# First expert table split by columns: 896 columns multiplied densely, 1152 gathered

## The chip, the core and the metric

One core of a Trainium2 chip runs the whole kernel in one launch. The metric is device time in microseconds (us), lower is better. All arithmetic is float32 (or fp32r, a float32 that PE reads in one pass).

## What is computed

A first block (retention, latent attention) and the attention of a second block come first; the change doesn't touch them. Behind them stands a mixture of 16384 experts, of which each of 256 tokens takes 8 heads x 16 picks = 128:

```python
q = (xt @ w_query).reshape(T, 8, 2, 128)
scores = jnp.einsum('thpc,hpnc->thpn', q, sub_keys)
vals, idx = lax.top_k(scores, 16)                      # per half: 16 of 128 keys
cand = (vals[..., 0, :, None] + vals[..., 1, None, :]).reshape(T, 8, 256)
top_vals, top_c = lax.top_k(cand, 16)
experts = i1 * 128 + i2                                # i1, i2: keys of the two halves
gates = softmax(top_vals)
# xc: tokens after rms_norm and gain
u = jnp.take(expert_down, experts, axis=0)             # rows of 2048
hdn = gelu(einsum('ted,td->te', u, xc))
vsel = jnp.take(expert_up, experts, axis=0)            # rows of 2048
y = einsum('te,ted->td', gates * hdn, vsel)
out = rms_norm(h + y)
```

## The kernel before

Tokens lie as two tiles t of 128 on the partitions. SP streams all weight matrices through eight 4 KB slots in the order of a list (`plan`); PE multiplies them as three fp32r products of high and low parts; ACT makes the high part, DVE the low one. Each engine's program is written out in order, with semaphores named for what was made (`x.at(key)` is waited for, `x.to(key)` is signalled). `take(b)` on PE waits until PSUM bank b is free.

The expert part, engine by engine:

**Selection.** PE multiplies queries with keys (`sel_scores`, L2200). ACT copies the scores to `SC`; the copy for tile 1 waits until tile 0 is ranked there. DVE ranks them (`top16`, `select`, L1584 to L1658) as a list of small steps, 147 and 150 counting the gates: 73 run before the first row, then two before each row. `chosen` releases the row numbers `EI` of 64 picks, L1649 ends a tile's selection.

**First table.** POOL gathers one pick of 128 tokens per instruction (L640): 128 rows of 2048 columns into one of NG = 8 buffers, for 256 picks. DVE multiplies each with `HN` (the normed tokens with gain) and sums it into a column of `HD[t]` (L1686). At the end of a tile ACT takes the gelu (L1024), DVE multiplies by the gates (L1691): `coef_made`.

**Second table, 896 columns (`DCOL`) by a dense product.** The coefficients of a tile are spread over all 16384 experts: PE turns `HD` (L2248), and for each group q of four tokens two one-hots of 128 are made, the first weighted by the coefficients, and multiplied with each other (`built`, L2258); ACT stores the result to `CO` (`store`, L1016). In tile 0 PE compares the picks' keys with 0..127 (two fp32r matmuls L2229 of 512 columns and two of one row, L2231) and ACT makes both one-hots (L1043 to L1053), beside the rows of tile 1. In tile 1 PE compares only the first key (L2229, L2231), DVE makes the first one-hot (L1707) after every second row of the second table, ACT the second (L1037, L1048). SP streams 128 blocks of 448 KB through NS = 4 slots, and PE multiplies each with both tiles' `CO` in four matmuls of 448 columns (L2275), once both tiles are stored.

**Second table, the other 1152 columns.** POOL gathers them (L651) into NU = 5 buffers; DVE adds coefficient times row to `X` (L1699), 256 rows one after another.

**End.** DVE adds the dense result (L1715), ACT squares, DVE scales, SP writes out.

Of the kernel before, what the change touches and what calls it, by code (L numbers as in the profile page):

```python
# [15 lines left out]
NG = 8  # L16
DCOL = 896
HCOL = DCOL // 2
NU = 5
# [15 lines left out]
K_ALL = 2066  # L35


def tables():
# [37 lines left out]
    t[:, K_STEP:K_ALL] = np.arange(128)  # L76
# [41 lines left out]
def build(nc, A, out):  # L118
    ctx = ExitStack()
    with ctx:  # L120
# [112 lines left out]
        HN = XN  # L233
        QT = at(YG + 4096, 16, 256)
        KT = at(W, 16, 128)
        SC = at(W + 2048, D)

        def column(o):
            cell = [o]

            def take_(*shape):
                a = at(cell[0], *shape)
                cell[0] += int(np.prod(shape))
                return a, cell[0]
            return take_

        scratch, kept = column(W + 4096), column(192 * KB + K_DM)
# [3 lines left out]
        WK, scratch_end = scratch(256)  # L251
        assert scratch_end <= 192 * KB, scratch_end
        II = [GBA[:, 128 * i:128 + 128 * i] for i in range(2)]
        IF = [GBA[:, 256 + 128 * i:384 + 128 * i] for i in range(2)]
        EI, GT, HD, CFT = ([kept(*n)[0] for _ in range(2)] for n in ((128,), (8, 16), (128,), (128,)))
        GS = kept(8)[0]
        G16, kept_end = kept(128)
        EF = [GBA[:, 512 + 256 * t:768 + 256 * t].rearrange("p (i j) -> p i j", i=2) for t in range(2)]
        EFR = [at(kept_end + 256 * t, 2 - t, 128, of=arena_r) for t in range(2)]
        SECOND = at(kept_end + 384, 128)  # L260
        STEP, LESS, IDR, ONER = (at(kept_end + 512 + 128 * i, 128, of=arena_r if i else arena) for i in range(4))
        assert kept_end + 1024 <= LBO + 4 * 384, kept_end
        gbuf = [at(RAWS + i * 2048, D) for i in range(NG)]

        ubuf = [at(W + 4096 + (D - DCOL) * i, D - DCOL) for i in range(2)] + [at(YG + (D - DCOL) * i, D - DCOL) for i in range(3)]
        sbuf = [at(144 * KB + DCOL * i, DCOL) for i in range(2)] + [at(W + 8192 - DCOL * i, DCOL) for i in (2, 1)]
        OH1 = [at(152 * KB + 512 * i, 4, 128) for i in range(2)]
        OH2 = [at(152 * KB + 1024 + 512 * i, 4, 128) for i in range(2)]

        CO = [[(0, 64, at(16 * KB, 64, 128)), (64, 32, at(YG + 4096, 32, 128)), (96, 32, at(W, 32, 128))],  # L270
              [(0, 64, at(RAWS, 64, 128)), (64, 64, at(HLS, 64, 128))]]

        def coef_of(t, i2):
            return next(ap[:, i2 - a, :] for a, n, ap in CO[t] if a <= i2 < a + n)

# [149 lines left out]
        d_g = [dma_sig(f"d_g{i}", range(32)) for i in range(NG)]  # L425
        d_u = [dma_sig(f"d_u{i}", range(52)) for i in range(NU)]
        d_s = [dma_sig(f"d_s{i}", range(43)) for i in range(NS)]
# [82 lines left out]
        sel_ranked = sig("sel_ranked", [(t, f) for t in range(2) for f in range(2)])  # L510
        chosen = sig("chosen", [(t, f) for t in range(2) for f in range(2)])
        gate_in, gate_exp, gate_made = sig("gate_in", range(2)), sig("gate_exp", range(2)), sig("gate_made", range(2))
        rows_used = sig("rows_used", range(512))
        gelud, coef_made = sig("gelud", range(2)), sig("coef_made", range(2))
        rounded, picks_rounded = sig("rounded", [0]), sig("picks_rounded", range(2))
        coef_turned, coef_copied = sig("coef_turned", range(2)), sig("coef_copied", range(2))
        fours = [(t, q) for t in range(2) for q in range(32)]
        first_hot_a, first_hot_v = sig("first_hot_a", fours[0:32]), sig("first_hot_v", fours[32:])
        compared, less_read, second_hot = sig("compared", fours), sig("less_read", fours), sig("second_hot", fours)
        second_turned, second_copied = sig("second_turned", [0]), sig("second_copied", [0])  # L520
        built, stored = sig("built", fours), sig("stored", fours)
        block_used = sig("block_used", range(127))
# [33 lines left out]
        down, up_rows, up_blocks = A["peer_down_2"][0], A["up_rows"], A["up_blocks"]  # L556


        def sync(sp):
# [22 lines left out]
            sp.wait_ge(*gate_made.at(1))  # L582
            sp.wait_ge(*picks_rounded.at(1))
            sp.wait_ge(*second_copied.at(0))
# [10 lines left out]
        def gpsimd(g):  # L595
# [33 lines left out]
            g.dma_start(GBB, A["ffn_norm_gain_2"][0].partition_broadcast(128)).then_inc(*d_ff.to("all"))  # L629
            g.dma_start(STEP, A["table"][:, K_STEP:K_ALL]).then_inc(*d_step.to("all"))  # L630
            g.dma_start(G16[0:16, :], A["final_norm_gain_2"].rearrange("(n p) -> n p", p=128)).then_inc(*d_f2.to("all"))

            g.wait_ge(*query_copied.at((3, 1)))
            for n in range(256):
                i, t, j = n % NG, n // 128, n % 128
                if j % 64 == 0:
                    g.wait_ge(*chosen.at((t, j // 64)))
                if n >= NG:
                    g.wait_ge(*rows_used.at(n - NG))
                g.indirect_dma_start(  # L640
                    out=gbuf[i], out_offset=None, in_=down,
                    in_offset=bass.IndirectOffsetOnAxis(ap=EI[t][:, j:j + 1].bitcast(U32), axis=0)
                ).then_inc(*d_g[i].to(n // NG))
            g.wait_ge(*gate_made.at(1))
            for n in range(256):
                i, t, j = n % NU, n // 128, n % 128
                if n == 2:
                    g.wait_ge(*rows_used.at(255))
# [8 lines left out]
        def scalar(s):  # L657
# [361 lines left out]
            for t in range(2):  # L1019
# [9 lines left out]
                for q in range(33):  # L1029
# [25 lines left out]
                    if q:  # L1055
                        store(t, q - 1)
# [1258 lines left out]
```

## Time and profile before

| | us |
|---|---|
| median of three runs | 3309.46 (3308.81 to 3310.41) |
| profiled execution, its own time | 3310.61 |
| its span | 3308.8 |
| PE busy | 2507.0 (76%) |
| DVE busy | 2292.5 (69%) |
| ACT busy | 1032.7 (31%) |
| POOL busy | 871.4 (26%) |

The core moved 866.75 MB, mean 262 GB/s. Times in the rows are us from the start of the span unless marked ns. PE is TensorE's matmuls, PEld its weight loads, DVE VectorE, ACT ScalarE, POOL GpSimd, SP the queue of SyncE. "Clock" is the share of 2.4 GHz that TensorE was granted. A float32 matmul leaves two records, an fp32r one leaves one. Durations of PE records include the way through the array; how often they come is read from their number in a stretch. A gather's duration on POOL is its issue alone.

### The profile page before, as it was taken

How to read it: one execution, taken by the hardware profiler on the slowest of the kernel's cores; microseconds unless marked ns; L12 is line 12 of the kernel's file. 1: busy time of each engine (PE TensorE's matmuls, PEld its weight loads, DVE VectorE, ACT ScalarE, POOL GpSimd, SP SyncE). 2: the span in 40 equal slices, each digit the busy share in tenths (PEclk: the TensorE clock that was granted, in tenths of full speed). 3: DMA queues.
4: the chain of work that ended last, by engine and by line, in shares of the span. 5: the costliest groups of instructions: out<-in, count | busy, mean ns of one | idle time of the engine just before them, and what ended most of it. 6: DMA issues, size and time to landing. Idle time of an engine off the chain costs nothing.

```text
span 3308.8 us, 34747 instructions
## 1 busy us (share of the span) xinstructions
PE 2507.0 (76%) x13253; PEld 2029.7 (61%) x13253; DVE 2292.5 (69%) x3034; ACT 1032.7 (31%) x1748; POOL 871.4 (26%) x581
## 2 busy tenths in 40 slices
PE   3689999998989998799999986000069106899995
PEld 3689999996879986698888786000036004655552
DVE  6877777776765455533435557999999898866666
ACT  2234343434344444443335442000058105400000
POOL 5510000000000000000000002833388786744444
PEclk9789999998989999799989988555555555599997
DMA  8767787775856534355333543999999998999998
GB/s 291 254 232 244 262 272 261 257 258 198 294 177 172 152 115 134 110 165 164 103 90 109 165 151 148 382 367 347 338 407 422 420 422 318 323 407 409 410 409 318
DMA packets 340694, 866.75 MB, mean 262 GB/s; under 512 B 38072, under 2 KB 97728, under 8 KB 306864
## 3 DMA queue, kind: packets, MB, share of 16 engines
q1 hardware_dynamic: 265872, 439.15, 40.1%
q0 software_dynamic: 74656, 425.38, 33.0%
q8 instruction: 105, 1.72, 0.2%
q14 instruction: 61, 0.50, 0.0%
HBM read 862.34 MB, written 2.10 MB: 261 GB/s over the span
## 4 chain that ended last, share of the span: by engine, by line
PE 35%; DVE 14%; DMA 12%; POOL 11%; issue 4%; ACT 1%; DVEq 0%; ACTq 0%; POOLq 0%
DMA s<-in_up_rows,s 10%; PE ps L1741 10%; PE ps L1742 10%; PE ps L1743 10%; POOL s L640 8%; DVE s L1686 7%; POOL s L651 3%; DVE s L1699 2%; DMA s<-in_peer_down,s 1%; PE ps L2119 1%; PE ps L2002 1%; PE ps L2121 1%; DVE s L1596 0%; DVE s L1587 0%; DVE s L1590 0%
## 5 line engine op out<-in xcount | busy, mean ns | idle before, releaser
L1741 PE MATMUL ps<-r,r 128*128 128x256 f32 (+2 forms) x3248 | 1063.9, 328 | 74.7 <-DVE r L1089 43.5
L1742 PE MATMUL ps<-r,r 128*128 128x256 f32 (+2 forms) x3248 | 1044.5, 322 | 0.0
L1089 DVE TENSOR_TENSOR r<-s,r 128x1024 fp32r<-128x1024 f32 (+1 forms) x532 | 647.3, 1223 | 572.9 <-ACT r L666 572.5
L1743 PE MATMUL ps<-r,r 128*128 128x256 f32 (+2 forms) x3248 | 1043.3, 321 | 0.0
L666 ACT CAST r<-s 128x1024 fp32r<-128x1024 f32 (+1 forms) x532 | 550.3, 1039 | 897.7 <-PE ps L1743 849.9
L1741 PEld LDWEIGHTS ps<-r,r 128*128 128x128 f32 x3248 | 639.9, 197 | 132.7 <-DVE r L1089 41.2
L1742 PEld LDWEIGHTS ps<-r,r 128*128 128x128 f32 x3248 | 640.4, 197 | 43.0 <-issue 4.6
L1743 PEld LDWEIGHTS ps<-r,r 128*128 128x128 f32 x3248 | 639.2, 197 | 41.0
L1686 DVE CUSTOM_DVE_ANT_0 s<-s,s 128x2048 f32<-128x2048 f32 x256 | 582.8, 2285 | 33.2 <-DMA s<-in_peer_down,s 33.0
L640 POOL DMA_INDIRECT s<-in_peer_down,s x256 | 464.8, 1816 | 409.6 <-DVE s L1644 189.3
L1699 DVE SCALAR_TENSOR_TENSOR s<-s,s,s 128x1152 f32<-128x1152 f32 x256 | 363.0, 1418 | 167.0 <-DMA s<-in_up_rows,s 162.9
L651 POOL DMA_INDIRECT s<-in_up_rows,s x256 | 305.0, 1191 | 253.4 <-DVE s L1699 205.7
L2275 PE MATMUL ps<-s,s 128*128 128x448 f32 x960 | 366.0, 542 | 0.0
L2229 PE MATMUL ps<-r 128*128 128x512 f32 x96 | 75.0, 781 | 353.8 <-ACT r L1010 353.8
L2275 PEld LDWEIGHTS ps<-s,s 128*128 128x128 f32 x960 | 183.3, 191 | 179.6 <-issue 179.6
L625 POOL DMA_DIRECT2D s<-in_final_norm_g x1 | 0.6, 625 | 1093.0 <-DVE s L1435 1093.0
L2229 PEld LDWEIGHTS ps<-r 128*128 128x128 f32 x96 | 30.5, 318 | 368.0 <-ACT r L1007 354.0
L1107 DVE SCALAR_TENSOR_TENSOR s<-s,s,s 128x512 f32<-128x512 f32 x304 | 226.8, 783 | 2.5 <-DMA s<-in_ada_w 1.1
L2248 PE MATMUL ps<-s 128*128 128x128 f32 x2 | 0.9, 448 | 202.5 <-DVE s L1691 202.5
L2258 PE MATMUL ps<-s 128*128 128x128 f32 x512 | 131.9, 439 | 27.9 <-issue 17.1
L2258 PEld LDWEIGHTS ps<-s 128*128 128x128 f32 x512 | 114.0, 328 | 56.9 <-ACT s L1016 29.3
L1060 ACT ACTIVATE s<-s 128x1152 f32<-128x1152 f32 x2 | 2.3, 1162 | 419.1 <-DVE s L1699 419.1
(266 smaller groups left out, 2033.7 us busy)
## 6 DMA issues: line engine op xcount, KB each, us to landing
s<-in_ada_w SPq DMA_DIRECT2D x192, 512.0 KB, 5.3
s<-in_ret_w_in SPq DMA_DIRECT2D x128, 512.0 KB, 5.2
s<-in_up_blocks SPq DMA_DIRECT2D x128, 448.0 KB, 6.8
s<-in_w_in SPq DMA_DIRECT2D x96, 512.0 KB, 3.7
s<-in_ret_w_in SPq DMA_DIRECT2D x128, 256.0 KB, 3.8
s<-in_ret_w_out SPq DMA_DIRECT2D x64, 512.0 KB, 5.0
s<-in_mla_w_in SPq DMA_DIRECT2D x48, 512.0 KB, 3.7
s<-in_mla_w_out SPq DMA_DIRECT2D x32, 512.0 KB, 3.6
```

The costliest lines, as they stand in the source:

```text
L640: g.indirect_dma_start(out=gbuf[i], out_offset=None, in_=down, in_offset=bass.IndirectOffsetOnAxis(ap=EI[t][:, j:j + 1].bitcast(U32), axis ...
L651: g.indirect_dma_start(out=ubuf[i], out_offset=None, in_=up_rows, in_offset=bass.IndirectOffsetOnAxis(ap=EI[t][:, j:j + 1].bitcast(U32), a ...
L666: s.copy(hi_of(w), raw_of(w)).then_inc(*hi_made.to(w))
L1089: v.tensor_tensor(lo_of(w), raw_of(w), hi_of(w).bitcast(F), ALU.subtract).then_inc(*lo_made.to(w))
L1107: r = v.scalar_tensor_tensor(out=acc[h], in0=w, scalar=cact[:, k:k + 1], in1=acc[h], op0=ALU.mult, op1=ALU.add)
L1686: v.tensor_tensor_reduce(gbuf[n % NG], gbuf[n % NG], HN[:, t, :], 1.0, 0.0, ALU.mult, ALU.add, HD[t][:, j:j + 1]).then_inc(*rows_used.to(n))
L1699: v.scalar_tensor_tensor(out=X[:, t, DCOL:], in0=ubuf[n % NU], scalar=HD[t][:, j:j + 1], in1=X[:, t, DCOL:], op0=ALU.mult, op1=ALU.add).th ...
L1741: pe.matmul(o, lh, rh, start=start, stop=False, skip_group_check=True)
L1742: pe.matmul(o, lh, rl, start=False, stop=False, skip_group_check=True)
L1743: return pe.matmul(o, ll, rh, start=False, stop=stop, skip_group_check=True)
L2258: r = pe.matmul(bank[b][:, k * 128:(k + 1) * 128], OH1[q % 2][:, k, :], OH2[q % 2][:, k, :], start=True, stop=True)
L2275: r = pe.matmul(bank[2 * t + b][:, 0:HCOL], coef_of(t, i2), sbuf[i2 % NS][:, b * HCOL:(b + 1) * HCOL], start=i2 == 0, stop=i2 == 127)
```

## The change

The first table is split like the second. `down_rows` holds columns 896 to 2047, `down_blocks` the other 896, as 128 blocks, one for each first key i1, laid out as [128 columns of a part, 7 parts, 128 second keys i2].

- **Dense product.** SP streams the 128 blocks through the four slots that later hold the second table's (now 256 blocks in a row; the first two wait for `hn_made`, the next two for the last scores). After the scores PE multiplies each with the normed tokens `XNT` (transposed, kept from the turning of "E"), 7 matmuls of 256 columns a block, two blocks a bank. ACT copies the result to `DH[i2, i1 group, token, i1]`, 64 copies.
- **Picks.** After the last copy, for each group q of four tokens of a tile: PE spreads the tokens' second keys over the partitions (`spread_`, four matmuls of 128 columns, one bank), ACT turns them into a one-hot (`pick_hot_`: Abs, Relu), PE multiplies it with the four tokens' slices of `DH` (`pick_rows`, four matmuls of 512 columns in all), so that each pick has its 128 values over i1, and DVE takes the one at its first key (`pick`, four operations on PSUM with a sum) into `SL`. PE turns `SL`, DVE adds it to `HD` (`hidden`), then gelu and gates as before.
- **Order.** DVE calls `pick` for tile 0 after rows 116 to 147, one a row, for tile 1 after rows 150, 153, ..., 243. PE runs tile 0's 32 groups after the dense product; in tile 1's loop it also builds tile 0's coefficients, three groups behind, with a single pair of one-hot buffers. ACT likewise.
- **Rows.** Gathers of both tables have 1152 columns. The first 56 use a ring of NA = 7 buffers, all later ones a ring of NB = 4. Row 56 waits for the end of selection. The second table's rows follow in the same ring.
- **Selection.** Five steps before each row; `SC` has a buffer for each tile; the gates are made after rows 64 and 100. `HNG`, the tokens times gain, has 1152 columns.

```diff
-NG = 8
-NU = 5
+GCOL = D - DCOL
+NA, EARLY, NB = 7, 56, 4
...
+        def before_row(n):
+            return n - NA if n < EARLY + NB else n - NB
+        PICK_AT = [116 + q for q in range(32)] + [150 + 3 * q for q in range(32)]
...
-            for b in range(128):
+            for b in range(256):
+                if b == 0:
+                    sp.wait_ge(*hn_made.at(1))
+                if b == 2:
+                    sp.wait_ge(*sel_scored.at((1, 3)))
                 if b >= NS:
                     sp.wait_ge(*block_used.at(b - NS))
-                sp.dma_start(sbuf[b % NS], up_blocks[b]).then_inc(*d_s[b % NS].to(b // NS))
+                sp.dma_start(sbuf[b % NS], down_blocks[I1_ORDER[b]] if b < 128 else up_blocks[b - 128]).then_inc(
+                    *d_block[b % NS].to(b // NS))
...
+            for q in pairs64:
+                if q in (20, 40):
+                    picks(q // 20 - 1)
+                s.wait_ge(*block_used.at(2 * q + 1))
+                if q == 32:
+                    s.wait_ge(*gate_in.at(1))
+                if q == 48:
+                    s.wait_ge(*rows_used.at(EARLY - 1))
+                i1 = I1_ORDER[2 * q]
+                s.copy(DH[:, i1 // 32, :, i1 % 32:i1 % 32 + 2], bank[4 + q % 4].rearrange("p (i t) -> p t i", i=2)).then_inc(
+                    *hid_stored.to(q))
+
+            def pick_hot_(t, q):
+                o = flat(PH[q % 2])
+                s.wait_ge(*spread.at((t, q)))
+                if fours.index((t, q)) >= 2:
+                    s.wait_ge(*rows_picked.at(fours[32 * t + q - 2]))
+                s.activation(o, bank[2], ACT.Abs, bias=NEG).then_inc(*spread_read.to((t, q)))
+                s.wait_ge(*spread_read.at((t, q)))
+                s.activation(o, o, ACT.Relu, scale=-1.0, bias=1.0).then_inc(*pick_hot.to((t, q)))
...
+            def pick(t, q):
+                if q == 0:
+                    v.wait_ge(*turned_read.at(t))
+                v.wait_ge(*rows_picked.at((t, q)))
+                for k in range(4):
+                    o, c = bank[3 + q % 2][:, k * 128:(k + 1) * 128], 4 * q + k
+                    r = v.scalar_tensor_tensor(out=o, in0=STEP, scalar=FIRST[t][:, c:c + 1], in1=o, op0=ALU.is_equal,
+                                               op1=ALU.mult, accum_out=SL[t][:, c:c + 1])
+                r.then_inc(*picked.to((t, q)))
...
             for n in range(256):
                 t, j = n // 128, n % 128
                 if n:
-                    next(choice, None)
-                    next(choice, None)
-                v.wait_ge(*d_g[n % NG].at(n // NG))
-                v.tensor_tensor_reduce(gbuf[n % NG], gbuf[n % NG], HN[:, t, :], 1.0, 0.0, ALU.mult, ALU.add,
+                    for _ in range(5):
+                        next(choice, None)
+                v.wait_ge(*d_row[row_slot(n)[1]].at(n))
+                v.tensor_tensor_reduce(row_buf(n), row_buf(n), HNG[:, t, :], 1.0, 0.0, ALU.mult, ALU.add,
                                        HD[t][:, j:j + 1]).then_inc(*rows_used.to(n))
+                if n in (64, 100):
+                    gates((64, 100).index(n))
+                if n == 148:
+                    hidden(0)
+                if n == 150:
+                    coefficients(0)
+                if n in PICK_AT:
+                    pick(*fours[PICK_AT.index(n)])
+            hidden(1)
+            coefficients(1)
...
+            for q in pairs64:
+                if q in (20, 40):
+                    turn_picks(q // 20 - 1)
+                take(4 + q % 4)
+                for j in range(2):
+                    b = 2 * q + j
+                    pe.wait_ge(*d_block[b % NS].at(b // NS))
+                    w = sbuf[b % NS].rearrange("p (k i) -> p k i", i=128)
+                    for k in range(DCOL // 128):
+                        r = pe.matmul(bank[4 + q % 4][:, j * 256:(j + 1) * 256], w[:, k, :], XNT[:, k, :],
+                                      start=k == 0, stop=k == DCOL // 128 - 1)
+                    r.then_inc(*block_used.to(b))
+                free[4 + q % 4] = hid_stored.at(q)
+
+            def spread_(t, q):
+                if q == 0:
+                    pe.wait_ge(*picks_rounded.at(t))
+                take(2)
+                for k in range(4):
+                    r = pe.matmul(bank[2][:, k * 128:(k + 1) * 128], IDR[:, 4 * q + k:4 * q + k + 1].broadcast_to([128, 128]),
+                                  EFR[t][:, 1, :], start=True, stop=True)
+                r.then_inc(*spread.to((t, q)))
+                free[2] = spread_read.at((t, q))
+
+            def pick_rows(t, q):
+                b = 3 + q % 2
+                take(b)
+                pe.wait_ge(*pick_hot.at((t, q)))
+                for k in range(4):
+                    c = 128 * t + 4 * q + k
+                    r = pe.matmul(bank[b][:, k * 128:(k + 1) * 128].rearrange("p (c i) -> p c i", c=4), PH[q % 2][:, k, :], DH[:, :, c, :], start=True, stop=True)
+                r.then_inc(*rows_picked.to((t, q)))
+                free[b] = picked.at((t, q))
...
             pe.wait_ge(*rounded.at(0))
...
+            pe.wait_ge(*hid_stored.at(63))
+            spread_(0, 0)
+            for q in range(32):
+                if q < 31:
+                    spread_(0, q + 1)
+                pick_rows(0, q)
+            spread_(1, 0)
+            for q in range(32):
+                if q < 31:
+                    spread_(1, q + 1)
+                pick_rows(1, q)
+                if q == 0:
+                    turn_picked(0)
+                if q == 2:
+                    turn_coef(0)
+                    compare(0, 0)
+                if q >= 3:
+                    build_(0, q - 3)
+                    compare(0, q - 2)
...
```

## Rows read from the trace of the kernel before

**Rows 1.** Busy time by stretch; busy us and (count) of each engine, clock, DMA.

```profile
core 0: us, PE busy (x) PEld busy (x) DVE busy (x) ACT busy (x) POOL busy (x), PEclk, DMA share, GB/s
1950.00:2000.00 50.00, 50.00 (x420) 50.00 (x420) 24.08 (x34) 20.07 (x24) 0.00 (x0) 1.00 0.57 179
2042.00:2745.00 703.00, 149.43 (x388) 92.15 (x388) 665.48 (x850) 136.85 (x368) 469.17 (x258) 0.50 0.98 386
2049.00:2389.00 340.00, 0.00 (x0) 0.00 (x0) 335.58 (x556) 2.25 (x5) 176.98 (x116) 0.50 0.96 362
2430.00:2590.00 160.00, 143.45 (x379) 89.76 (x379) 146.66 (x131) 128.31 (x347) 136.10 (x66) 0.50 1.01 421
2745.70:2880.10 134.40, 108.67 (x352) 79.53 (x352) 119.25 (x104) 78.47 (x225) 105.34 (x74) 0.50 0.91 314
2880.10:3267.50 387.40, 387.40 (x1025) 195.42 (x1024) 240.54 (x171) 1.25 (x2) 180.16 (x169) 0.99 1.02 406
2900.00:2950.00 50.00, 50.00 (x134) 25.27 (x133) 29.79 (x21) 0.00 (x0) 19.24 (x22) 1.00 1.02 408
```

**Rows 2.** Groups by line from 2000 us to the end.

```profile
L1686 DVE DVE_READ_ACCUMULATOR2_ANT s<- 128x1 f32 x256 | 21.1, 82 | 0.0
L1707 DVE SCALAR_TENSOR_TENSOR s<-ps,s 128x512 f32<-128x512 f32 x32 | 21.9, 684 | 0.0
L1691 DVE TENSOR_TENSOR s<-s 128x128 f32<-128x128 f32 x2 | 0.6, 294 | 0.8 <-ACT s L1024 0.8
```

**Rows 3.** Single lines: count, shortest/median/longest ns, first and last start.

```profile
L2200 PE MATMUL ps<-s,s x64: 272/275/341, 1989.2 to 2036.6; 128*128 128x128 f32 x64
L640 POOL DMA_INDIRECT s<-in_peer_down,s x256: 935/2170/3010, 2043.2 to 2726.2; - x128
L1649 DVE TENSOR_TENSOR s<-s x2: 293/294/294, 2161.7 to 2388.9; 128x128 f32<-128x128 f32 x2
L1686 DVE CUSTOM_DVE_ANT_0 s<-s,s x256: 2239/2289/2353, 2049.2 to 2742.6; 128x2048 f32<-128x2048 f32 x128
L1699 DVE SCALAR_TENSOR_TENSOR s<-s,s,s x256: 1407/1419/1454, 2745.8 to 3291.5; 128x1152 f32<-128x1152 f32 x128
L2275 PE MATMUL ps<-s,s x960: 539/539/1115, 2880.1 to 3267.0; 128*128 128x448 f32 x192
```

**Rows 4.** Issue to landing (last, us): 2760 to 2875, then 2900 to 3200.

```profile
s<-in_up_rows,s POOLq DMA_INDIRECT x63, 6.6
...
s<-in_up_blocks SPq DMA_DIRECT2D x100, 448.0 KB, 6.8
s<-in_up_rows,s POOLq DMA_INDIRECT x131, 9.7
```

**Rows 5.** PE alone, two pauses: busy us (records), clock, DMA share, GB/s.

```profile
1252.00:1254.00 2.00, 0.07 (x1) 1.00 0.65 218
...
1274.00:1276.00 2.00, 0.00 (x0) 0.50 0.57 225
```

**Rows 6.** Timeline of one group of four in the first tile: PE, then ACT.

```profile
2432.32 0.77 PE L2229 MATMUL ps<-r 128*128 128x512 f32 x1
...
2435.19 2.08 PE L2258 MATMUL ps<-s 128*128 128x128 f32 x8
2436.92 0.77 PE L2229 MATMUL ps<-r 128*128 128x512 f32 x1
...
2435.30 0.60 ACT L1043 ACTIVATE s<-ps 128x512 f32<-128x512 f32 x1 [0.73 <-PE ps L2231]
...
2436.42 0.63 ACT L1047 ACTIVATE s<-s 128x512 f32<-128x512 f32 x1
...
2437.60 1.28 ACT L1053 ACTIVATE s<-s,s 128x128 f32<-128x128 f32 x4
2438.78 0.68 ACT L1016 COPY s<-ps 128x256 f32<-128x256 f32 x3
```

**Rows 7.** Timeline: first one-hot of the second tile.

```profile
2754.23 0.68 DVE L1707 SCALAR_TENSOR_TENSOR s<-ps,s 128x512 f32<-128x512 f32 x1
```

More of the change, by code:

```diff
@@ L267, in build @@
[L267 to L274, printed above, removed]
+        WK = scratch(256)[0]
+        II = [scratch(128)[0] for _ in range(2)]
@@ L1595, in top16 @@
                 v.wait_ge(*steps.at())
[L1596 removed]
+                v.max_index(idx[:, 8:16], val[:, 8:16], wk).then_inc(*steps.to())
                 yield
@@ L2219, in tensor, with turn_picks @@
                         sel_scores(t, g)
-            def compare(t, q):
+            def turn_picks(t):
+                pe.wait_ge(*chosen.at((t, 1)))
+                take(t)
+                for p in range(2):
+                    r = pe.transpose(bank[t][:, p * 128:(p + 1) * 128], EF[t][:, p, :], IDN)
+                r.then_inc(*picks_turned.to(t))
+                free[t] = turned_read.at(t)
+            for q in pairs64:
[11 more added lines that the diff above has]
+                free[4 + q % 4] = hid_stored.at(q)
@@ new lines, in turn_coef, with compare @@
+            def turn_coef(t):
+                take(5)
+                pe.wait_ge(*coef_made.at(t))
+                pe.transpose(bank[5][:, 0:128], HD[t], IDN).then_inc(*coef_turned.to(t))
+                free[5] = coef_copied.at(t)
+            def compare(t, q):
+                if t:
+                    b = q % 2
+                    if q == 0:
+                        take(0)
+                        take(1)
+                    take(b)
+                    hs = [(b, 0)]
+                else:
+                    hs = [(0, 0), (1, 1)]
+                    take(0)
+                    take(1)
+                for b, p in hs:
@@ new lines, in compare, with build_ @@
+                for b, p in hs:
+                    free[b] = first_hot_v.at((1, q)) if t else less_read.at((0, q))
+            def build_(t, q):
+                b = 6 + q % 2
+                take(b)
+                pe.wait_ge(*(first_hot_v if t else first_hot_a).at((t, q)))
+                pe.wait_ge(*second_hot.at((t, q)))
+                o1, o2 = (OH1[q % 2], OH2[q % 2]) if t else (OH1[0], OH2[0])
+                for k in range(4):
+                    r = pe.matmul(bank[b][:, k * 128:(k + 1) * 128], o1[:, k, :], o2[:, k, :], start=True, stop=True)
+                r.then_inc(*built.to((t, q)))
+                free[b] = stored.at((t, q))
@@ L2262, in tensor @@
+            for q in (29, 30, 31):
+                build_(0, q)
+                if q < 31:
+                    compare(0, q + 1)
+            turn_picked(1)
+            turn_coef(1)
+            compare(1, 0)
+            for q in range(32):
+                if q < 31:
+                    compare(1, q + 1)
+                build_(1, q)
             for b in range(4, 8):
```

308 lines of the change are left out of this document (153 added, 155 removed).

## The prediction

> **What bounds the kernel now.** I read the busy table by stretches first [rows 1]. Until 2037 us of the span it is projections and attention, which the change leaves alone. Then PE stops and the expert part begins: from 2042 to 2745 the core gathers whole 8 KB rows of the first expert table, DMA busy 0.98 at 386 GB/s, PE idle or at half clock. From 2745.7 to 2880 the first 1152-column rows of the second table are added while PE builds the second token tile's coefficients at clock 0.50. From 2880 to 3267 PE multiplies the 896-column blocks and is busy in every microsecond, with the DMA share at 1.02 and 406 GB/s: there both are full. The groups by line [rows 2] give prices, the sources' first and last starts [rows 3] the marks: gather issue begins at 2043.2, the second tile's selection ends at 2388.9 (L1649), the last first-table row starts on DVE at 2742.6, the first second-table row at 2745.75 (L1699), dense product 2880.1 to 3267, last row 3291.5. So the first-table stretch is limited by DMA (2.49 us a row late in it, by DVE steps before) and everything behind it hangs on one mark: **the moment T at which the coefficients of both tiles exist, now 2745.7.** From T to the end of the span it is 3308.8 - 2745.7 = 563.1 us. The change rewrites what comes before T and little behind it, so I compute the new T.
>
> **Bytes.** Removed: 256 gathers x 128 rows x 896 columns x 4 B = 117 MB. Added: 128 blocks of 448 KB = 59 MB. Net 58.7 MB less; at 386 GB/s that is 152 us, the most this can give if DMA stayed the bound. It does not: the rest of the sum is PE's.
>
> **Dense first product.** 128 blocks x 7 float32 matmuls with 256 moving columns. In the dense stage now, 134 records of 448 columns stand in 50 us [rows 1], 373 ns a record, two records a matmul: 0.833 ns per column and record. So 256 columns cost 427 ns, 896 matmuls 382 us, 2.99 us a block. What could hide or stall it: the scores end on PE at 2036.9 [rows 3], blocks 0 and 1 are loaded before, 2 and 3 land some 5 us later, in time. A slot comes round after three blocks, 9 us, against 6.8 us to landing [rows 4] beside saturated queues. The copies (64 of 512 columns, 0.68 us as three pieces in L1016's row [rows 6]) fit beside. Its 153 GB/s leaves the rows some 250 GB/s. PE comes from full clock (2.4 GHz), and the clock stays at 1.00 over a short gap: in [rows 5] PE worked 0.07 us of the two from 1252 on, and kept it; in a longer pause it had lost it by 1274. Weight loads lie beside the stream in [rows 1], 25 of 50 us. Dense ends at 2037 + 382 = 2419. In the Trainium skill, "TensorE: Matmul & The Clock Gate", section "What overlaps and what doesn't", a weight load overlaps running matmuls only where the row group differs; our loads take all rows, so by it this stage would be longer. The trace disagrees for this kind of matmul: 373 ns is two times 448 columns at 2.4 GHz with nothing between.
>
> **DVE and rows meanwhile.** 5 selection steps go before each row instead of 2; 221 steps remain. Now they and 110 rows take 2049 to 2389: 340 - 110 x (2.29 + 0.08) = 79 us for the steps; a little DMA wait is hidden in there, and as the steps' cost alone stands in no one row I take 92 between that and a third more, 105. With 45 rows of 1152 columns at 1.44 us (bounds: 2.29 x 1152/2048 = 1.29 and the 1.42 of L1699, plus 0.08 for reading the sum out) the selection is done near 2049 + 65 + 92 = 2206, before the copy that waits for it (pair 32, 2233). Rows then go at 2.3 us beside the stream; row 116, where DVE meets the first pick, comes near 2370. There it waits for PE until 2423: row gathers stop with it, and this is where the saved bytes go unused.
>
> **Picks of the first tile.** All on PE after the dense product. From its end to the first pick product: last copy 0.6, spread 0.5, Abs 0.6 and Relu 0.63 on ACT [rows 6] and hops, 3.5 us: 2423. Each group of four is 4 float32 matmuls of 512 columns: 4 x 853 = 3.41 us. The spread (4 matmuls fp32r of 128 columns) is not in the trace: below, 4 x 0.12 (the 256-column fp32r record, 420 in 50 us [rows 1]) = 0.5; above, 4 x 0.72 (the compare's cadence at half clock [rows 6]) = 2.9. I take 0.5, since it is the same array form as the former, without the one-row matmul between. So 3.9 us a group. ACT (1.2) and DVE (one row 1.44 + four picks) lie beside it; a pick is a 128-column operation on PSUM: below 4 x 0.29 (L1691, [rows 2]) = 1.2, above 4 x (0.68 + 0.08) = 3.1 from L1707 [rows 2]; I take 1.5. 32 x 3.9 = 125: 2548. Rows move one per group, 151 GB/s of the 406 possible.
>
> **Picks of the second tile, with the first tile's coefficients.** Three groups pass before the one-hots join (12 us) plus 4 us for transpose, gelu and coefficient copy one after another: 2564. Then per group PE does pick 3.41, spread 0.5, build 0.85 (8 records of 128 columns; 1.71 us at half clock [rows 6]), compare. The compare costs 2.87 us at half clock [rows 6], 0.72 a matmul, of which 0.43 is columns and 0.29 exposed load; at full clock 0.21 + 0.19, so 1.6. A hop to ACT's last one-hot copy adds 0.25: **6.6 us**. ACT needs 3.6 (from the first Abs at 2435.30 to the last copy's end at 2438.88 [rows 6]) + 0.6 + 1.2 = 5.4, DVE 3 x 1.44 + 1.5 = 5.8, both inside. 29 x 6.6 = 191: 2755. Twelve rows remain, four of them ready: 12 x 1.6 = 19; last pick, transpose, gelu and product 3 to 5. **T = 2779**, 33 us later than now. PE alone (382 + 125 + 191) already fills that stretch.
>
> **Behind T.** The same loops. Ring of 4 buffers for 5: in the one-hot stretch rows land 6.6 us after issue (median [rows 4]), so (6.6 + 1.42 + 0.1)/4 = 2.03 us a row against the present 1.87 (134.4 us for 72): at most 12 us; less if the queue in front is shorter. Against it, four rows lie ready at T, where now the first one-hot waits for late rows until 8.5 us after T [rows 7]. I put both together at nothing. In the dense stretch DMA is full whatever the ring. The store has one copy for two: nothing. Dropped norm columns, table loads: under 2 us, nothing.
>
> **Sum.** Span 3308.8 + 33 = 3342, and the profiled execution took 3310.6 for its 3308.8: 3344. It stood 1.2 us over the median of three, 3309.5, inside their spread, so I do not correct.
>
> **Rivals.**
> *Not slower: the loads hide at full clock (0.25).* If the compare costs its columns alone (0.85), a group takes 3.41 + 0.5 + 0.85 + 0.85 + 0.25 = 5.9, T is 2564 + 171 + 24 = 2759, and PE, still at full clock, leaves the later one-hot stretch to DVE (2 x 1.42 + 0.68, so 3.5 instead of 3.73 us a group, -7) with rows ready (-6): 3311; with a group of 3.6 in the first tile (-10) and the last rows at 1.44 (-2), 3299. It decides from T under 2751. For it: loads hide in the fp32r stream. Against: they did not in the compare, busy without a gap [rows 6]. Faster 0.15, same 0.10.
> *The ring of four limits the rows (0.12).* Now 9.7 us to landing + 1.42 + 0.3 make 11.4 for five, 2.28 a row. If landing stays 9.7, four give 2.85; 171 rows x 0.57 = 97 more: 3441. Against: the DMA share of 1.02 says that time is queueing, which shrinks with the depth.
> *Half clock in the picks (0.06).* A group is then 7.3 and 12.2 us (6.83 + 1.7 + 2.87 + 0.6 and a hop): 2423 + 234 + 26 + 354 + 24 = 3061, the run 3626. For it: the one-hot stretches are busy 0.9 of the time at 0.50 and never rise [rows 1]. Against: PE comes in at 1.00, and the picks are the dense product's kind. In the Trainium skill the same page's "Loop structure matters more than you think" warns that a wait between bursts makes PE run cold; here the bursts wait about 0.3 us.
> *Loads stand in front of the dense matmuls (0.02).* Where the load of 0.19 us is exposed at each of 1792 records, 340 us more: 3684. That is the skill's overlap rule taken literally; 373 ns a record speaks against it.
>
> **Numbers.** My forecast has 0.55, at 3344, its own range 3318 to 3380. A measurement here tells 0.2%, 6.6 us, from no change. Faster 0.15; same 0.10; slower 0.75, of which 0.55, 0.12, 0.06 and 0.02. The range leaves out the two dear cases, the dear end of the ring case and the low end of the cheap one: 3296 to 3430.
>
> **What would show it.** Right: PE busy from 2037 at clock 1.00 with 427 ns a matmul to 2420; DVE idle from near row 116 until then, DMA near 150 GB/s from 2350 to 2550; pick groups 3.9 and then 6.6 us apart; first second-table row near 2779; 563 us from there. Wrong: picks under 6 us apart (rival one), more than 2.4 us a row in the dense stretch (two), clock 0.50 between 2420 and 2755 (three), a dense first product of over 400 us (four).

## The result and the profile after

The changed kernel takes **3370.28 us** (median of four runs, 3367.53 to 3372.58) against 3309.93 for the kernel before in the same session: ratio 1.0182, 95% interval 1.0165 to 1.0200. It is slower by 60 us where 3344 had forecast 35 more than before; the range given, 3296 to 3430, holds it. The profiled execution took 3371.31 us for a span of 3369.4. Two of the third experiment's four runs fell in a slower state (4928.92 and 5827.68 us; one run of the kernel before did so too, 5181.67), so its time below is that of the other two and stands without an interval.

The core moved 807.97 MB, 58.8 less than before. PE is busy 3042.0 us (90%, before 76%), DVE 2130.7 (63%, before 69%). The moment T, at which the first second-table row starts on DVE, is 2781.8 (before 2745.7, forecast 2779). From T to the end of the span it is 587.6 us (before and forecast 563.1). So 36.1 us were lost ahead of T and 24.5 behind it.

The busy table by stretches, after, answers to [rows 1]. The stretches are the dense first product, its last 20 us but four, the picks of tile 0, the loop over tile 1 in its steady part, the one-hots behind T, the dense second product, and the rows left over.

```profile
core 0: us, PE busy (x) PEld busy (x) DVE busy (x) ACT busy (x) POOL busy (x), PEclk, DMA share, GB/s
2037.00:2424.40 387.40, 387.40 (x1799) 341.63 (x1798) 256.15 (x576) 42.80 (x77) 125.07 (x121) 1.00 0.91 338
2400.00:2420.00 20.00, 20.00 (x94) 17.66 (x93) 0.00 (x0) 2.41 (x4) 0.00 (x0) 1.00 0.47 143
2429.20:2504.60 75.40, 57.49 (x381) 53.48 (x381) 75.40 (x320) 41.90 (x64) 29.03 (x31) 0.86 0.79 236
2513.00:2752.80 239.80, 214.80 (x685) 156.35 (x684) 153.45 (x431) 149.47 (x317) 116.76 (x93) 0.50 0.68 227
2781.80:2928.10 146.30, 110.04 (x353) 80.08 (x353) 119.80 (x104) 76.68 (x193) 91.39 (x71) 0.50 0.84 279
2928.10:3315.70 387.60, 387.60 (x1025) 196.01 (x1024) 235.68 (x167) 1.25 (x2) 159.36 (x166) 0.99 1.01 400
3315.70:3354.00 38.30, 0.00 (x0) 0.00 (x0) 26.29 (x20) 0.31 (x1) 20.44 (x16) 0.54 0.78 257
```

PE is full in the first line, at clock 1.00, and the loads (341.63 us) lie beside the stream. In the second line DVE and POOL do nothing, and DMA moves 143 GB/s: the stall before the first pick. Then DVE is busy in all of the 75.40 us of tile 0's picks. In the tile-1 loop the clock (PEclk) has fallen to 0.50, PE has work in 214.80 of 239.80 us, DVE in 153.45, and DMA moves 227 GB/s: the saved bytes bought nothing here. Behind T, the fifth line answers to 2745.70:2880.10 in [rows 1]: 146.3 us for 134.4, at 279 GB/s for 314. The dense second product is as long as before (387.6 for 387.4). The last line is longer than its counterpart: the last row starts 36.5 us after the dense product, before 24.0 [rows 3].

Single lines, after: count, shortest/median/longest ns, first and last start. L2321 is the dense first product, L2344 the pick product, L1742 the pick on DVE, L1763 a row of the first table (before L1686), L1781 one of the second (before L1699).

```profile
L2321 PE MATMUL ps<-s,s x1792: 378/380/383, 2037.2 to 2424.2; 128*128 128x256 f32 x200
L2344 PE MATMUL ps<-big,s x512: 274/421/583, 2427.4 to 2751.3; 128*128 128x128 f32 x171
L1742 DVE SCALAR_TENSOR_TENSOR ps<-s,ps x256: 346/355/360, 2429.2 to 2752.5; 128x128 f32<-128x128 f32 x128
L1763 DVE CUSTOM_DVE_ANT_0 s<-s,s x256: 1339/1356/1421, 2049.3 to 2773.8; 128x1152 f32<-128x1152 f32 x128
L1781 DVE SCALAR_TENSOR_TENSOR s<-s,s,s x256: 1407/1418/1486, 2781.8 to 3352.2; 128x1152 f32<-128x1152 f32 x128
```

1792 records of the dense product in 387.3 us are 216 ns each, 432 ns a matmul. The pick product has 128 moving columns, not 512. The row reduction takes 1.36 us.

Issue to landing, after (median us), in the one-hots (2785 to 2925) and in the dense second product (2935 to 3250), answering to [rows 4]:

```profile
s<-in_up_rows,s POOLq DMA_INDIRECT x69, 5.9
...
s<-in_up_rows,s POOLq DMA_INDIRECT x136, 7.5
```

The end of the stall, from the timeline of the kernel after (start, us, engine, line; in brackets the idle time before and what ended it):

```profile
2429.18 0.35 DVE L1742 SCALAR_TENSOR_TENSOR ps<-s,ps 128x128 f32<-128x128 f32 x1 [62.87 <-PE ps L2344]
2429.45 0.14 DVE L1742 DVE_READ_ACCUMULATOR ps<-s,ps 128x1 f32 x1
2429.45 0.35 DVE L1742 SCALAR_TENSOR_TENSOR ps<-s,ps 128x128 f32<-128x128 f32 x1
...
2430.26 1.35 DVE L1763 CUSTOM_DVE_ANT_0 s<-s,s 128x1152 f32<-128x1152 f32 x1
...
2431.89 0.94 POOL L674 DMA_INDIRECT s<-in_down_rows,s  x1 [64.37 <-DVE s L1763]
```

DVE had waited 62.87 us for the first pick product, POOL 64.37 for DVE to free a row. Four picks start 0.27 us apart (2429.18, 2429.45, ...) though each is recorded with 0.35 and 0.14: 1.08 us for four.

One steady group of the tile-1 loop, same view. L2375 and L2377 are the compare, L1076 to L1084 tile 0's one-hots on ACT, L2389 the build, L2344 the pick product:

```profile
2604.74 0.78 PE L2375 MATMUL ps<-r 128*128 128x512 f32 x1
...
2606.89 0.79 PE L2377 MATMUL ps<-r 1*128 1x512 f32 x1
...
2607.72 0.60 ACT L1076 ACTIVATE s<-ps 128x512 f32<-128x512 f32 x1 [3.06 <-PE ps L2377]
...
2608.52 2.02 PE L2344 MATMUL ps<-big,s 128*128 128x128 f32 x8
...
2610.01 1.28 ACT L1084 ACTIVATE s<-s 128x128 f32<-128x128 f32 x4
...
2611.39 2.05 PE L2389 MATMUL ps<-s,s 128*128 128x128 f32 x8 [0.85 <-issue]
...
2613.09 0.77 PE L2375 MATMUL ps<-r 128*128 128x512 f32 x1
```

The way round is a chain. Compare 2604.74 to 2607.6, four matmuls at 0.72 us; ACT's Abs starts at 2607.72, after waiting 3.06 us for the last of them; the scaled one-hots end at 2611.29; the build's eight records start at 2611.39; and only behind them comes the next compare, 2613.09. That is **8.35 us a group**. The picks (2608.52, 2.0 us) lie beside ACT's part and are on no edge of it. PE works 7.50 us of the 8.35, and DVE is idle 3.35 us of each group. The kernel before had no such chain. It keeps two pairs of one-hot buffers and issues the next compare ahead of the build, so in [rows 6] compare, build and compare follow each other on PE without a pause, 4.60 us a group (2432.32, 2436.92), at the same clock of 0.50.

The tail before T, same view:

```profile
2773.82 1.36 DVE L1763 CUSTOM_DVE_ANT_0 s<-s,s 128x1152 f32<-128x1152 f32 x1 [0.35 <-DMA s<-in_down_rows,s]
...
2778.47 2.05 PE L2389 MATMUL ps<-s,s 128*128 128x128 f32 x8 [3.71 <-ACT s L1084]
...
2780.31 0.42 PE L2351 MATMUL ps<-s 128*128 128x128 f32 x1
...
2780.84 0.29 DVE L1750 TENSOR_TENSOR s<-s,ps 128x128 f32<-128x128 f32 x1 [5.65 <-PE ps L2351]
...
2781.83 2.94 DVE L1781 SCALAR_TENSOR_TENSOR s<-s,s,s 128x1152 f32<-128x1152 f32 x2
```

The last row of the first table is reduced by 2775.1, but PE is still at tile 0's last build; DVE waits 5.65 us for the turned picks behind it.

### The profile page after: what moved, and what is told of

The parts are those of the page before. It is cut to its first block, busy times and chain, and to the rows that moved or that the text cites. A ratio compares the mean times of both kernels' runs of the same rounds, so it can differ in the third digit from the quotient of the medians.

```text
span 3369.4 us, 40821 instructions
## 1 busy us (share of the span) xinstructions
PE 3042.0 (90%) x15818; PEld 2508.4 (74%) x15818; DVE 2130.7 (63%) x3548; ACT 1148.6 (34%) x1847; POOL 662.5 (20%) x580
## 2 busy tenths in 40 slices
DMA packets 359153, 807.97 MB, mean 240 GB/s; under 512 B 40120, under 2 KB 99776, under 8 KB 358192
## 4 chain that ended last, share of the span: by engine, by line
PE 54%; DMA 13%; DVE 6%; issue 3%; ACT 2%; POOL 1%; DVEq 0%; ACTq 0%
DMA s<-in_up_rows,s 13%; PE ps L2321 11%; PE ps L1823 10%; PE ps L1824 10%; PE ps L1825 10%; DVE s L1781 3%; PE ps L2389 2%; PE ps L2344 2%; PE ps L2377 1%; PE ps L2375 1%; DVE s L1763 1%; DVE ps L1742 1%; PE ps L2333 1%; POOL s L674 1%; PE ps L2201 1%
## 5 line engine op out<-in xcount | busy, mean ns | idle before, releaser
L1823 PEld LDWEIGHTS ps<-r,r 128*128 128x128 f32 x3248 | 642.3, 198 | 133.4 <-DVE r L1147 40.5
L1781 DVE SCALAR_TENSOR_TENSOR s<-s,s,s 128x1152 f32<-128x1152 f32 x256 | 363.3, 1419 | 190.4 <-DMA s<-in_up_rows,s 187.7
L674 POOL DMA_INDIRECT s<-in_down_rows,s x256 | 285.5, 1115 | 630.3 <-DVE s L1763 411.1
L1763 DVE CUSTOM_DVE_ANT_0 s<-s,s 128x1152 f32<-128x1152 f32 x256 | 342.4, 1355 | 81.8 <-DMA s<-in_down_rows,s 81.6
L2437 PE MATMUL ps<-s,big 128*128 128x448 f32 x1024 | 387.5, 542 | 0.0
L2321 PE MATMUL ps<-s,s 128*128 128x256 f32 x1792 | 387.3, 380 | 0.0
L2321 PEld LDWEIGHTS ps<-s,s 128*128 128x128 f32 x1792 | 341.1, 190 | 45.3
L2437 PEld LDWEIGHTS ps<-s,big 128*128 128x128 f32 x1024 | 196.0, 192 | 191.0 <-issue 190.9
L674 POOL DMA_INDIRECT s<-in_up_rows,s x256 | 275.8, 1077 | 301.8 <-DVE s L1781 282.3
L1742 DVE SCALAR_TENSOR_TENSOR ps<-s,ps 128x128 f32<-128x128 f32 x256 | 74.3, 354 | 140.5 <-PE ps L2344 140.5
L1046 ACT COPY big<-ps 128x512 f32<-128x512 f32 x64 | 39.1, 611 | 344.4 <-PE ps L2321 344.4
L2389 PE MATMUL ps<-s,s 128*128 128x128 f32 x384 | 98.3, 438 | 55.2 <-issue 38.8
```

Source lines behind the costliest of these rows:

```text
L674: g.indirect_dma_start(out=row_buf(n), out_offset=None, in_=down_rows if n < 256 else up_rows, in_offset=bass.IndirectOffsetOnAxis(ap=EI[t ...
L1763: v.tensor_tensor_reduce(row_buf(n), row_buf(n), HNG[:, t, :], 1.0, 0.0, ALU.mult, ALU.add, HD[t][:, j:j + 1]).then_inc(*rows_used.to(n))
L1781: v.scalar_tensor_tensor(out=X[:, t, DCOL:], in0=row_buf(256 + n), scalar=HD[t][:, j:j + 1], in1=X[:, t, DCOL:], op0=ALU.mult, op1=ALU.add ...
L1823: pe.matmul(o, lh, rh, start=start, stop=False, skip_group_check=True)
L2321: r = pe.matmul(bank[4 + q % 4][:, j * 256:(j + 1) * 256], w[:, k, :], XNT[:, k, :], start=k == 0, stop=k == DCOL // 128 - 1)
L2389: r = pe.matmul(bank[b][:, k * 128:(k + 1) * 128], o1[:, k, :], o2[:, k, :], start=True, stop=True)
```

## The experiments

The theory had two parts. **S**: the tile-1 loop is set by the serial chain compare, ACT, build, at half clock. **R**: what was lost behind T is the ring of four. Rivals: **R'**, the loss behind T comes from the change's other edits there; **S'**, late rows set the loop, DVE meeting each pick after three of them.

Each ratio is to the runs of the kernel before in the same session: 3308.98 us for experiments 1 to 4, 3311.19 for 5 and 7. T and the time behind it are those of the profiled execution.

| kernel | median us | ratio to before | T | T to end |
|---|---|---|---|---|
| before | 3309.93 | | 2745.7 | 563.1 |
| after | 3370.28 | 1.0182 (1.0165 to 1.0200) | 2781.8 | 587.6 |
| 1: before, ring of 4 | 3338.65 | 1.0091 (1.0073 to 1.0109) | 2745.1 | 591.7 |
| 2: after, ring of 6 | 3325.15 | 1.0052 (1.0034 to 1.0070) | 2776.0 | 547.1 |
| 3: after, compare first | 3320.6 | | 2728.8 | 589.8 |
| 4: after, picks later | 3370.00 | 1.0183 (1.0165 to 1.0202) | 2777.2 | 590.8 |
| 5: 2, 3 and 4 together | 3266.99 | 0.9873 (0.9856 to 0.9889) | 2715.2 | 547.8 |
| 6: after, no picks | 3316.51 | (one run) | 2720.8 | 593.9 |
| 7: ring of 6, no compare in tile 0 | 3244.33 | 0.9802 (0.9785 to 0.9818) | 2690.5 | 549.5 |

**1. The kernel before with a ring of four.**

```diff
-NU = 5
+NU = 4
...
```

> The kernel before with four instead of five buffers for the second table's rows, nothing else. Theory R (the 24.5 us that the changed kernel loses behind the moment T when the coefficients exist come from its ring of four): first-table part unchanged, T stays at 2745.7, from T to the end 587 us instead of 563, so about 3334 us. Rival R' (they come from the other edits behind T, such as the storing of the coefficients): within 3 us of 3310.

Measured 3338.65, ratio 1.0091 (1.0073 to 1.0109). T stands at 2745.1, the whole loss is behind it: 591.7 for 563.1, 28.6 us. Its one-hot stretch, and its landing times in the dense stretch:

```profile
2745.10:2893.40 148.30, 108.62 (x352) 79.49 (x352) 118.55 (x103) 78.46 (x225) 95.21 (x72) 0.50 0.85 279
...
s<-in_up_rows,s POOLq DMA_INDIRECT x124, 7.5
```

The stretch is 148.3 us at 279 GB/s, like after's 146.3 at 279. In the dense product rows land after 7.5 us where five buffers gave 9.7 [rows 4]. The last row starts at 3319.5, 38.6 us behind the end of the dense product. So the ring by itself costs as much as all that the change lost behind T (28.6 us for 24.5); R' falls.

**2. After, with a ring of six for the second table.** The two further buffers lie in `HNG`, free after row 255; ACT's square at the end writes elsewhere.

```diff
-NA, EARLY, NB = 7, 56, 4
+NA, EARLY, NB, NC = 7, 56, 4, 6
...
+        cbuf = bbuf + [HNG[:, i, :] for i in range(NC - NB)]
...
+            if n >= 256:
+                return 2, (n - 256) % NC
...
+            if n >= 256 + NB:
+                return 255 if n < 256 + NC else n - NC
...
```

> The changed kernel with a ring of six for the second table's rows: the two further buffers lie where the tokens times gain stood, and are filled once the last first-table row is used. Theory R: from T to the end falls from 587.6 to 563 us or a little less, T stays near 2782, so 3345 us or some us under it, and the last row ends under 28 us after the dense product, against 36.5. Rival R': stays within 5 us of 3370.

Measured 3325.15. From T to the end 547.1, which is 40.5 under after and 16.0 under before: R had expected 563 or a little less, so six buffers give more than back what four took. The first stretch below is in the tile-1 loop, the second the one-hots; then the landing in the dense product:

```profile
2600.00:2700.00 100.00, 89.78 (x289) 65.64 (x288) 59.75 (x169) 62.34 (x132) 44.42 (x37) 0.50 0.63 213
2776.00:2899.70 123.70, 110.09 (x353) 80.08 (x353) 118.97 (x106) 76.71 (x193) 99.67 (x72) 0.50 0.93 333
...
s<-in_up_rows,s POOLq DMA_INDIRECT x142, 12.1
```

The one-hots take 123.7 us at 333 GB/s, and the last row starts 18.8 us behind the dense product (3305.9 against 3287.1). The landing grew to 12.1 us: with full queues a deeper ring only waits longer; it gains where DMA was not full. The loop before T is what it was, 0.50. T came 5.8 us earlier with nothing edited ahead of it, and in run 4 4.6 earlier. Of the 5.8, 2.6 were there before the dense first product began (2034.6 against 2037.2), and the rest came by the handover between the tiles; why is not shown, and none of the verdicts needs it.

**3. Compare ahead of build.** PE issues the next group's compare before the build that waits for ACT; nothing is added or taken away.

```diff
                 if q >= 3:
-                    build_(0, q - 3)
                     compare(0, q - 2)
+                    build_(0, q - 3)
```

> The changed kernel; in the second tile's pick loop PE runs the next group's comparison ahead of the build of the group before, instead of behind it. Theory S (a group of 8.35 us is a serial chain: comparison 2.87, hop, ACT 3.5, hop, build 1.71, all at half clock): the comparison then runs beside ACT, PE's own work of 7.4 us bounds the group, 32 groups give 27 us, T near 2755, 3343 us. Rival S' (rows: the gathers that stood still from 2366 to 2429 are what is late): no change, 3370 us.

Measured 3320.4 and 3320.9, 50 us under after, with T 53 earlier, twice what S had expected. The last pick is at 2703.5, after's at 2752.5. Below are the loop's steady part, two groups at half clock, one at full clock, the build of that one with what follows it on PE, and one compare at full clock:

```profile
2580.00:2700.00 120.00, 102.10 (x448) 75.89 (x446) 97.41 (x269) 96.92 (x210) 74.26 (x58) 0.74 0.86 284
2559.75:2574.07 14.32, 14.32 (x50) 10.82 (x50) 11.22 (x30) 10.40 (x23) 8.41 (x6) 0.50 0.89 285
2602.63:2607.81 5.18, 4.31 (x26) 3.12 (x24) 3.40 (x7) 5.08 (x12) 4.37 (x3) 0.99 0.86 278
...
2606.29 1.13 PE L2389 MATMUL ps<-s,s 128*128 128x128 f32 x8 [0.74 <-issue]
2607.30 0.76 PE L2333 MATMUL ps<-r 128*128 128x128 f32 x4
...
2656.01 0.46 PE L2375 MATMUL ps<-r 128*128 128x512 f32 x1
...
2656.40 0.49 PE L2377 MATMUL ps<-r 1*128 1x512 f32 x1
...
2656.83 0.48 PE L2375 MATMUL ps<-r 128*128 128x512 f32 x1
...
2657.24 0.49 PE L2377 MATMUL ps<-r 1*128 1x512 f32 x1
```

ACT's first Abs of group 0 starts at 2512.0 and that of group 28 at 2689.9, so a group takes 6.35 us on average, for 8.35. The expectation was 7.4 at half clock; but the clock did not stay there. It is 0.74 over 2580 to 2700, where after showed 0.50, although PE was busy 102.10 of 120 us, a smaller share than after's 214.80 of 239.80. The last four lines are one compare at full clock: its matmuls start 0.39 to 0.43 us apart, at half clock 0.72. The trace tells the order's part from the clock's. Where the clock is 0.50, two groups take 14.32 us, 7.16 each, and PE has no pause: that is what S expected. Where it is 1.00, a group takes 5.18, PE works 4.31 of it and ACT 5.08, so ACT's work is then the bound. Between the two stand groups of 7.6 to 9.6 us; in one of them PE waits 1.71 us for DVE's picks. At 7.16 throughout, the 28 groups would have taken 200.5 us for the 177.9 measured, so by this estimate most of the 26 us beyond the expectation is the clock.

**4. Picks eleven rows later.**

```diff
-        PICK_AT = [116 + q for q in range(32)] + [150 + 3 * q for q in range(32)]
+        PICK_AT = [127 + q for q in range(32)] + [161 + 3 * q for q in range(32)]
```

> The changed kernel with every pick on DVE 11 rows later (127 to 158, then 161 to 254 in threes), so that rows go on while PE still works on the dense product and one row instead of 12 remains behind the last pick. Rival S' (rows are late): the stall at the first pick shrinks from 63 to under 40 us and T comes 15 to 20 us earlier, 3350 us. Theory S: T hangs on PE, which still has three groups to build when the rows are done; no change beyond 4 us, the wait of DVE for the turned picks grows from 5.65 to over 20 us, 3366 to 3370 us.

Measured 3370.00, ratio 1.0183 (1.0165 to 1.0202): no change against after. DVE's waits between 2360 and 2800 (total us, times, longest):

```profile
DVE ps L1742 <- PE ps L2344: 106.9, 23, 35.0
DVE s L1763 <- DMA s<-in_down_rows,s: 27.5, 27, 1.8
DVE s L1750 <- PE ps L2351: 26.7, 1, 26.7
```

The stall before the first pick fell from 62.9 to 35.0 us, and 26.7 came back as a wait for the turned picks at the tail. Rows were further along at every pick and nothing ended sooner, so rows do not set the loop; S' falls. The stall, the most visible idle time of the profile, was worth nothing as long as the chain stood.

**5. Ring, order and picks together.**

> The changed kernel with the three edits of the last runs together: ring of six, comparison ahead of the build, picks 11 rows later. With the comparison first, T was 2728.8 and DVE no longer waited for PE but PE for the last 12 rows (25 us); now one row is left there. Theory S: the later picks, worth nothing alone, now give 10 to 20 us: T 2710 to 2718, and 547 us behind it as with the ring of six alone: 3258 to 3268 us. Rival S' (rows stay late whatever the order of picks): T stays near 2729, 3278 us.

Measured 3266.99, ratio 0.9873 (0.9856 to 0.9889). T is 2715.2, 66.6 earlier than after; the three alone moved it by 5.8, 53.0 and 4.6, together 63.4. Against run 3 it is 13.6 earlier, inside the 10 to 20 that S had expected of the later picks once the chain is out of the way. Behind T it is 547.8, as in run 2. The loop, and DVE's two waits between 2500 and 2716:

```profile
2580.00:2700.00 120.00, 101.08 (x443) 74.34 (x444) 98.37 (x273) 97.35 (x210) 78.49 (x58) 0.77 0.86 283
...
DVE s L1769 <- DMA s<-in_down_rows,s: 34.7, 45, 1.6
...
DVE s L1756 <- PE ps L2357: 12.6, 1, 12.6
```

The clock is 0.77, DVE waits for rows 34.7 us in 45 pieces, and at the end 12.6 for PE. Over the whole stretch no single resource is full; as in run 3 the bound changes with the clock, and groups of 5.2 us at 1.00 stand beside groups of 7.16 and more at 0.50.

**6. After without the picks.** All 64 pick groups are left out on PE, ACT and DVE, so the 896 columns' share of the hidden values is missing; dense product, rows and coefficients stay.

> The changed kernel without the 64 groups of picks (no spread, no one-hot for it, no pick product, no pick on DVE; the 896 columns' share of the hidden values is left out), everything else and its order kept. Theory S (comparison, ACT, build, comparison in a serial chain at half clock sets the group, not the pick work): the first tile's coefficients exist near 2445, the building loop starts there and still takes 8.0 to 8.4 us a group, T near 2715. If pick work shared in the bound: under 7.4 us a group, T under 2690. If rows bound T: T near 2690 with DVE waiting for DMA, not for PE.

Measured 3316.51 in one run. Two builds in a row in the loop, and the loop by stretch:

```profile
2600.17 2.05 PE L2383 MATMUL ps<-s,s 128*128 128x128 f32 x8 [3.71 <-ACT s L1084]
...
2608.53 1.83 PE L2383 MATMUL ps<-s,s 128*128 128x128 f32 x7 [3.71 <-ACT s L1084]
...
2451.50:2720.00 268.50, 149.05 (x386) 91.29 (x386) 143.85 (x211) 127.77 (x289) 140.34 (x106) 0.50 0.71 237
```

The group starts at 2600.17 and again at 2608.53: 8.36 us, the same as with the picks, while PE's work in a group fell from 7.5 us (214.80/239.80 of 8.35) to 4.6 (149.05/268.50 of 8.36), and PE now waits 3.71 us for ACT before each build. The clock is 0.50 in both. So in after the picks of tile 1 were free, and the chain at that clock set the group: S holds. T is 2720.8 because the loop started 61.5 us earlier.

**7. The chain taken apart.** With run 2's ring. In tile 0 PE compares nothing: DVE makes the weighted one-hot, ACT the other from a bias, as tile 1 has it. The picks come at rows 140 to 171 and 174 to 250, and PE turns tile 1's picks ahead of the last three builds; what each of these is worth by itself was not tried.

```diff
-        PICK_AT = [116 + q for q in range(32)] + [150 + 3 * q for q in range(32)]
+        PICK_AT = [140 + q for q in range(32)] + [174 + 76 * q // 31 for q in range(32)]
...
+            def hot(q):
+                v.wait_ge(*(built.at((0, q - 1)) if q else coef_copied.at(0)))
+                for k in range(4):
+                    c = 4 * q + k
+                    r = v.tensor_scalar(OH1[0][:, k, :], STEP, FIRST[0][:, c:c + 1], CFT[0][:, c:c + 1], ALU.is_equal, ALU.mult)
+                r.then_inc(*first_hot_a.to((0, q)))
...
                 if q == 2:
                     turn_coef(0)
-                    compare(0, 0)
                 if q >= 3:
                     build_(0, q - 3)
-                    compare(0, q - 2)
```

> Ring of six; no comparison on PE for the first tile: DVE makes the weighted first one-hot with four scalar operations a group (is_equal, mult; some 0.2 us each), ACT the second from the token's key as a bias, as in the second tile; picks from row 140 on, then in 2.45 rows a group, the last three groups' one-hots between the last rows. Theory S: PE is left with 4.5 us a group even at half clock, ACT 3.9, DVE bounds with 5.3 to 5.6: 32 groups from 2512 give T near 2685 and 3234 us. Rival (the saved chain shows another of its length, through the single pair of one-hot buffers): 7 us a group or more, T over 2730, 3278 us or more.

Measured **3244.33**, ratio 0.9802 (0.9785 to 0.9818), 126 us under after and 66 under before. T is 2690.5, 5.5 us behind the expectation, and the time 10 over it; the rival, T over 2730, falls. A stretch of the loop, and DVE's one-hot:

```profile
2500.00:2660.00 160.00, 103.39 (x564) 96.72 (x562) 154.18 (x491) 99.67 (x221) 95.16 (x74) 0.71 0.82 270
...
L1751 DVE TENSOR_SCALAR s<-s x128: 334/344/551, 2520.1 to 2686.0; 128x128 f32<-128x128 f32 x128
```

DVE is busy 154.18 of 160 us, PE 103.39, DMA moves 270 GB/s: the bound has gone to DVE, which now does rows, picks and one-hots. The time against before comes from both sides of T: 55.2 us ahead of it and 13.6 behind.

## Why the prediction was right, and where it was not

The direction is right, the time to 26 us, T to 3 us. T's agreement is an accident of two terms.

- **Dense first product: right.** 427 ns a matmul forecast, 432 measured, 382 us and 387. It ended at 2424.4, 5 us late. Loads hidden, as [rows 1] said; the fourth rival (3684) is dead. By the Trainium skill, "TensorE: Matmul & The Clock Gate", section "What overlaps and what doesn't", loads that take all rows would not overlap; at 216 ns a record with a load of 190 in each, the trace disagrees for this kind of matmul.
- **DVE and rows meanwhile: right.** The selection ended with L1705 at 2206.3 (2206), the idle time began near row 116 at 2366 (2370), DMA ran at 143 GB/s then (153). In tile 0's picks it ran at 236, where 151 was forecast: a row every 2.35 us instead of every 3.9.
- **Picks of the first tile: mis-sized.** "4 float32 matmuls of 512 columns: 4 x 853 = 3.41 us" was misread: the 512 columns are those of all four together. Each has 128, under 1.2 us a group (in the tile-1 loop 2.02 at half clock). The stretch was DVE's, a row and four picks of 0.27: 75.4 us for 125, **50 less**. A DVE pick cost 1.08 for four, under my 1.5.
- **Handover: 8.4 us for 16**, 2504.6 to 2513, where the first compare starts.
- **Picks of the second tile: wrong in its mechanism.** I added PE's work at full clock, 6.6 us a group. The chain behind the compare sets 8.35 at clock 0.50 (run 6), 239.5 us for 191, **49 more**. Two steps failed. One is the sentence "a hop to ACT's last one-hot copy adds 0.25": ACT's 3.6 us are not inside the group but between compare and build, since both one-hots have one buffer and PE's order puts the next compare behind the build. The prices came from [rows 6], where two pairs of buffers and the other order let them add up on PE alone; the change gave up both. The other is the clock, put at 1.00 where 0.50 was measured. The way round of 8.35 is 2.98 from the compare's start to ACT's, 3.67 to the build's and 1.70 to the next compare's. At full clock run 3's lines make it, by an estimate, 1.75 + 3.67 + 1.01 = 6.4, no more than the 6.6 that I had; and PE's own work at half clock is 7.5. So neither explains the 49 us alone: 0.9 us a group is PE's work at half clock over my sum, itself swollen by the misread pick, and 0.85 is the pause that the chain adds to it. With the pick sized rightly and all else as I had it, DVE would have been the busiest engine of both stretches (2.9 us and 5.8 us a group), and the sum 2423 + 32 x 2.9 + 16 + 29 x 5.8 + 24 = 2724 for T, 3289 for the run: a forecast of faster. The first error hid the second.
- **Tail: 29.3 us for 24**, 2752.5 to 2781.8. The rows took 22.6, and PE, 5.65 us behind them, the rest.
- **Behind T: a term put at nothing that was 24.5.** The bound for the one-hots, 2.03 us a row for 72 rows, was met: 146.3/72 = 2.03, 11.9 us more. What was set against it, four rows lying ready, saves its waits once, while the longer round is paid at every row. The other 12.5 us stand behind the dense product and were in no term: four more rows are left over there, and the 17 go at 2.15 us each instead of 1.85 for 13. In the dense product itself the queueing argument nearly held: landing fell to 7.5, and 387.6/167 = 2.32 us a row against 2.27. It is these 0.05 us a row that leave the four rows over.
- **The rivals.** The ring (3441) does cost, but in the wrong place for this rival: 24.5 us, most of it where DMA is not full, not 97 in the dense stretch. Half clock in the picks (3626) came true for tile 1's loop alone, where the clock was 0.50 all through, and that is half of the loss there; its price was of the same misread 512 columns. "PE comes in at 1.00" held for the first tile (0.86 on average) and no further. Loads hidden in the compare (3311) did not occur; at full clock, in run 3, its four matmuls start 0.39 to 0.43 us apart, as my 1.6 for four had it.

## What to carry to other kernels

Before adding up an engine's work in a loop, follow one group from its first instruction to the same one of the next through every wait and every single buffer; a way round longer than the busiest engine's work sets the time. A price read from a loop holds for that loop's order and buffers; the order of two independent pieces of work on PE was worth 50 us of 3370 here, together with the clock that rose with it. A shorter ring costs little where the queues are full (0.05 us a row here) and its whole round trip where they are not, so price it stretch by stretch, the drained end included. A long idle time in front of a first instruction is a symptom: moving work into it (run 4) only moved the wait.

## What the runs showed of the hardware

- A float32 matmul with 256 moving columns and a new full-array load before each of its two records ran at 216 ns a record over 387 us, all loads (190 ns) hidden. The compare's fp32r matmuls, where a load of 128 rows alternates with one of a single row, start 0.72 us apart at half clock and 0.41 at full, where 512 columns alone are 0.43 and 0.21; the 0.29 more at half clock is the length of a load's record there (0.28), so the load seems not to be hidden.
- TensorE's clock stayed at 0.50 in a loop where PE was busy 214.80 of 239.80 us (after), and in run 6 at 149.05 of 268.50. In the kernel before it did so where PE had no pause in 120 us (tile 0's one-hots, line below). It stood at 0.74 to 0.77 in the reordered loops at 102.10 and 101.08 of 120; there it changed between 0.50 and 1.00, and rose behind two groups without a pause (14.32 of 14.32 us). The share of busy time doesn't order these; what does was not found.

```profile
2438.00:2558.00 120.00, 120.00 (x314) 74.14 (x313) 112.39 (x99) 106.93 (x288) 104.76 (x51) 0.50 1.01 422
```

- Gathers of 128 rows of 4.5 KB with 4, 5 and 6 in flight: 7.5, 9.7 and 12.1 us to landing beside the block stream, at nearly the same rate (401 to 410 GB/s in all); without it 5.9, 6.6 and 6.7, and 279, 314 and 333 GB/s.
- A DVE pick on 128 columns of PSUM with a sum is recorded with 355 ns and 144 for the readout, yet four follow each other at 270 ns.
